# A two-block transformer kernel: the order of the four query blocks of each pair of heads, 128, 256, 384, 512 keys against 512, 128, 384, 256

## The reference, cut to what matters

```python
def fox_attention(q, k, v, log_f):
    ...
        s = jnp.einsum('bqhd,bkhd->bhqk', q_i, k).astype(jnp.float32) * scale
        s = s + c_i[..., :, None] - c_keys[:, :, None, :]
        s = jnp.where((k_pos[None, :] <= q_pos[:, None])[None, None], s, NEG_INF)
        p = jax.nn.softmax(s, axis=-1)
        return jnp.einsum('bhqk,bkhd->bqhd', p.astype(v.dtype), v)

def chunked_rel_attention(q, k, v, rel_bias):
    ...
    s = s + bias[None, :, None]
    s = jnp.where(valid[None, None, :, None, :], s, NEG_INF)
    p = jax.nn.softmax(s, axis=-1)
    o = jnp.einsum('bhnqk,bnkhd->bnqhd', p.astype(v.dtype), v_band)
```

## Time and profile before

| what | value |
|---|---|
| median of 3 runs | 1558.02 us (1558.0 to 1559.74) |
| profiled execution | 1563.09 us, span in the trace 1561.3 us |
| TensorE matmul busy | 1515.5 us, 97% of the span |
| VectorE, ScalarE, GpSimd busy | 54%, 39%, 15% of the span |
| stage of the 32 blocks on TensorE | from 157.2 us to 253.7 us of the span |

### The profile page before, as it was taken

The page is one execution under the profiler, slowest core; times in us unless marked ns, Lnnn a source line. Parts: engine busy times, 40 slices in busy tenths (PEclk is TensorE's granted clock), DMA queues, the critical chain, the costliest instruction groups (busy, mean ns, idle before and its releaser), DMA issues.

```text
span 1561.3 us, 21409 instructions
## 1 busy us (share of the span) xinstructions
PE 1515.5 (97%) x7988; PEld 1235.7 (79%) x7988; DVE 850.1 (54%) x1104; ACT 602.0 (39%) x923; POOL 240.3 (15%) x266
## 2 busy tenths in 40 slices
PE   9999988999998999999999899999999999999998
PEld 6787667887887888888888588888887788888887
DVE  6433564527545543433323786756876776767323
ACT  6222554643244322222323543335764433333222
POOL 0200000024014100000000554554542000000000
PEclk9999899999999999999999999999999999999999
DMA  5532002431112223333232123222002333232321
GB/s 166 190 97 92 1 2 64 153 108 54 55 55 81 81 81 107 93 96 108 81 107 90 50 77 108 81 98 91 2 1 82 96 91 107 81 107 82 109 105 54
DMA packets 152809, 132.22 MB, mean 85 GB/s; under 512 B 6300, under 2 KB 137628, under 8 KB 152740
## 3 DMA queue, kind: packets, MB, share of 16 engines
q1 hardware_dynamic: 150836, 128.11, 26.5%
q0 software_dynamic: 848, 3.17, 0.6%
q10 hardware_dynamic: 1056, 0.00, 0.0%
HBM read 129.15 MB, written 2.12 MB: 84 GB/s over the span
## 4 chain that ended last, share of the span: by engine, by line
PE 85%; DVE 5%; POOL 3%; ACT 3%; issue 3%; DMA 0%; ACTq 0%; SPq 0%; DVEq 0%; POOLq 0%
PE ps L1797 25%; PE ps L1798 25%; PE ps L1799 25%; PE ps L2048 2%; POOL other_stats L774 2%; PE ps L2161 1%; POOL x_t L722 1%; PE ps L2143 1%; PE ps L459 1%; PE ps L2058 1%; DVE a_lo L1281 1%; PE ps L1985 1%; ACT work L914 1%; PE ps L2014 0%; ACT w_hi L800 0%
## 5 line engine op out<-in xcount | busy, mean ns | idle before, releaser
L1797 PE MATMUL ps<-a_hi,w_hi 128*128 128x512 f32 (+2 forms) x1656 | 645.4, 390 | 14.8 <-DVE a_lo L1281 5.7
L1799 PE MATMUL ps<-a_hi,w_lo 128*128 128x512 f32 (+2 forms) x1656 | 639.9, 386 | 0.0
L1798 PE MATMUL ps<-a_lo,w_hi 128*128 128x512 f32 (+2 forms) x1656 | 639.8, 386 | 0.0
L1797 PEld LDWEIGHTS ps<-a_hi,w_hi 128*128 128x128 f32 (+1 forms) x1656 | 311.3, 188 | 87.9 <-issue 10.2
L1799 PEld LDWEIGHTS ps<-a_hi,w_lo 128*128 128x128 f32 (+1 forms) x1656 | 311.5, 188 | 64.0
L1798 PEld LDWEIGHTS ps<-a_lo,w_hi 128*128 128x128 f32 (+1 forms) x1656 | 311.6, 188 | 62.1 <-issue 0.7
L800 ACT ACTIVATE w_hi<-raw 128x2048 fp32r<-128x2048 f32 x118 | 225.8, 1913 | 348.5 <-PE ps L1799 346.4
L1233 DVE TENSOR_TENSOR w_lo<-raw,w_hi 128x2048 fp32r<-128x2048 f32 x94 | 215.3, 2290 | 245.0 <-ACT w_hi L800 244.7
L727 POOL TENSOR_TENSOR w_lo<-raw,w_hi 128x2048 fp32r<-128x2048 f32 x24 | 110.6, 4609 | 452.9 <-ACT w_hi L800 452.9
L1654 DVE TENSOR_TENSOR arena<-ps,rstd 128x512 f32<-128x512 f32 x88 | 60.2, 689 | 166.3 <-PE ps L1799 159.9
L1724 DVE RECIPROCAL rstd<-std 128x512 f32<-128x512 f32 x24 | 80.5, 3353 | 26.3 <-ACT std L1147 26.3
(11 more groups left out here) (242 smaller groups left out, 1459.3 us busy)
## 6 DMA issues: line engine op xcount, KB each, us to landing
raw<-in_w_gate_up SPq DMA_DIRECT2D x44, 512.0 KB, 4.6
raw<-in_ffn_w_up SPq DMA_DIRECT2D x44, 512.0 KB, 4.6
raw<-in_attn_w_in SPq DMA_DIRECT2D x36, 512.0 KB, 4.4
raw<-in_w_in SPq DMA_DIRECT2D x24, 512.0 KB, 4.7
raw<-in_w_down SPq DMA_DIRECT2D x22, 512.0 KB, 4.0
raw<-in_ffn_w_down SPq DMA_DIRECT2D x22, 512.0 KB, 4.0
raw<-in_w_mem_kv SPq DMA_DIRECT2D x16, 512.0 KB, 4.2
raw<-in_w_out SPq DMA_DIRECT2D x8, 512.0 KB, 3.9
```

What stands on the lines that cost most here:

```text
L1797: pe.matmul(dst, s_hi, m_hi, start=start, stop=False, skip_group_check=across)
L1798: pe.matmul(dst, s_hi, m_lo, start=False, stop=False, skip_group_check=across)
L1799: return pe.matmul(dst, s_lo, m_hi, start=False, stop=stop, skip_group_check=across)
```

## The change

One line decides which query block a number b stands for. Before, the four numbers of a pair of heads stand for i = 0, 1, 2, 3; now for i = 3, 0, 2, 1. Everything else of a block (keys, PSUM region, bias slice, place of the result) follows from i and moves with it; banks and slots still follow b.

```diff
             def __init__(self, b):
-                self.b, self.decays, self.p, self.i = b, b < 16, b % 16 // 4, b % 4
+                self.b, self.decays, self.p, self.i = b, b < 16, b % 16 // 4, (3, 0, 2, 1)[b % 4]
                 self.n, self.slot = (self.i + 1) * 128, 2 * (b % 2)
```

## The result

The changed kernel takes 1565.82 us (median of 5 runs, 1564.69 to 1566.54) against 1558.02 us of before (5 runs, 1557.78 to 1559.74): a ratio of 1.0045, 95% interval 1.003 to 1.006. It is slower by 7.8 us in this comparison; in a second one by 5.6 us (1565.82 against 1560.27, ratio 1.0038, 1.0025 to 1.0052, 23 runs of before from 1557.41 to 1564.23). I had forecast 1559.2, no measurable change, and a range up to 1562.3: wrong.

A forecast was written before the change was run, and what follows sets the result against it. TensorE, busy 97%, was taken to bound the kernel: bias pairs lose 1.5 us, decays pairs gain 0.2, head, middle and tail gain 0.1, so 1.2 us later, 1559.2 us from a median of 1558.02; range 1556.4 to 1562.3.

The forecast's parts named there:

- What bounds the stage, and the intervals: TensorE bounds; intervals from a block's scores (S) to the preceding block's values (V) each lose 0.11 us.
- the walk: TensorE's timeline reckoned piece by piece: decays pair 11.64 us (gain 0.09), bias pair 11.17 us (loss 0.49).
- V0's new wait: Bias pairs: values of the 128-key block wait some 0.8 us on ACT's copy, which they did not before.
- The mechanism: Two long intervals that ran side by side now stand in a row: 3.79 + 4.58 of a bias pair's 11.17 us.
- the head of the stage: Stage start: 512-key scores first, at low clock until 168.1 us; first transposes at 162.5, first pair takes 19.35 us.
- head, middle and tail together: Stage's first pair, pair between decays and bias, and last pair: together to gain 0.1 us.
- the rival of the early clock: Head of the stage: clock rises at about 161 us and stays, 1.2 us faster than before, 1556.8; chance 0.17.
- The rival of the low clock: Stage: clock stays low longer or falls again in longer waits, 4.6 us per low bias pair, 1563.8; chance 0.14.

The follow-up runs named there:

- Swap32: Kernel before with block order 128, 256, 512, 384 keys in both halves: 1560.19 us, ratio 0.9998.
- from128: Kernel before with block order 128, 384, 256, 512 keys, the changed kernel's cycle begun with its 128-key block: 1565.71 us, ratio 1.0027.
- before_2: The kernel before, unchanged, traced again: 1560.96 us.
- before_warm: Kernel before plus ten unread matmuls of 512 columns in TensorE's two gaps ahead of the stage: 1559.82 us, ratio 0.9992.
- rot: Kernel before with block order 256, 384, 512, 128 keys, the same cycle begun one block later: 1559.69 us, ratio 1.0002.
- again: The changed kernel, unaltered, run once more beside the kernel before: 1565.82 us, ratio 1.0038.
- filled pair: Kernel before and changed kernel, both with unread matmuls ahead of the stage and where V waits: 1557.72 and 1563.87 us.
- after_fed: Changed kernel plus unread matmuls: ten ahead of the stage, eight ahead of the first transposes, three to five where V waits: 1563.87 us, ratio 1.0021.
- after_3: The changed kernel, unaltered, traced again: 1564.76 us.
- before_fed: Kernel before plus unread matmuls: ten ahead of the stage, one ahead of the first transposes, three where V waits: 1557.72 us, ratio 0.9995.
- mix: Kernel before with order 128, 256, 512, 384 keys in the decays half and 256, 384, 512, 128 in the bias half: 1559.3 us, ratio 0.9991.

## Why the prediction was wrong

*What bounds the stage, and the intervals: right.* Each price of the walk came out. Predicted and measured: S2 to V0 with the bias 3.79 and 3.79, S3 to V1 4.58 and 4.58, with decays 3.99 and 4.00, 4.85 and 4.85; a decays pair 11.64 and 11.66, the pair between the halves 11.37 and 11.41, a bias pair 11.17 and 11.20, from the last T3 to `mem_k` 10.15 and 10.18. Only the first T3 came earlier than reckoned, 4.6 us behind the first scores and not 5.3. V0's new wait was to be 0.8 and is 0.79, V1's 1.6 and is 1.60.

*The mechanism: right, and tested.* Swap32, which keeps the two big scores in neighbouring steps, has bias pairs of 10.9 to 11.0 us; from128, another start of the changed cycle, has 11.20.

*The step that failed is the head of the stage,* and with it the sum. I took the low clock of the earlier trace rows, 158.0 to 168.1, as a property of the place and gave the changed kernel the same one; 253.69 us, with which I compared, held 10 us of it. The other traces show that it is one launch's: none, 3.4, 6.8 or 10.2 us in that place. Without it before needs about 92.6 us for the stage (before_2 has 94.0, less 0.64 in its pair of 11.32 us and 0.74 in its tail, both under low clock; before_warm, with none, has 92.7, rot 92.5) and the change 94.8 (again has 96.3, less 1.55 up to its second pair, which took 17.83 us where 4.62 to the first T3 and one pair of 11.66 make 16.28). So the order costs 2.2 us and not 1.2; in the filled pair 2.8 with the filling's 0.6. In the prediction's terms: the bias pairs lose 1.5 us and the decays pairs gain 0.2, as reckoned, but head, middle and tail together were to gain 0.1 and lose about 0.8 at the upper level. The low clock made the head of before, cheap at the upper level, look 3.8 us dearer in the one trace that I had. The same step turned the rival of the early clock round: its first pair is about right (16.9 us reckoned, 16.4 in after_fed), but it was set against a before at low clock, and so came out 1.2 us faster where the order is 2.2 us slower. That the head's 19.35 us met 19.27 in the first trace after is luck: the stretch of low clock was 6.8 us there and not 10, it lay at 164 to 171, and the first T3 came 0.7 us earlier.

*The rival of the low clock: right in kind.* The clock did fall inside the stage behind the longer waits, in stretches of 3.4 us that cost 1.1 to 1.6 us each (a bias pair of 12.26 in place of 11.20 in the first trace after, 12.79 in after_3), not for a whole pair of heads at 4.6 us. Seven traces with the new bias cycle and its waits unfilled hold 8 low stretches behind 210 us (one, in from128, of 10 us), eight with another bias order 3. That points to the waits as a cause, but swap32 waits 1.54 us in V1 and has none, so it isn't shown. The mean over the traces above, 3.3 us between L2022 and L1797, takes in 2.2 of order and 1.1 of clock.

*The range failed for a second reason.* The three runs of before that I had were 1.7 us apart; 23 were 6.8 us apart. My base of 1558.02 us was the median of three launches among the quickest; that of 23 is 1560.27. Of the 6.6 us between my 1559.2 and the measured 1565.82, then, 2.3 lie in the base, 1.0 in the stage (2.2 for 1.2), 2.0 go with the lower clock of the change's launches, which my sum had at nothing (the low clock was a rival, at 0.14), and 1.3 stay open.

*What stays open.* The medians stand 5.6 us apart. 2.2 us are the order's, at the upper level. Another 2.0 go with granted clock, 0.9916 against 0.9937 on average, and with it goes the spread, 6.8 us over the launches of before and 2 over ten of the change: nine of the 23 launches of before ran at 0.996, and none of the change's above 0.993. Why the change's launches never reached that is not shown; the fed pair has the same, six of eleven launches of before_fed at 0.997, none of after_fed above 0.996. That a shift of 2 to 3 us moves later gaps to where the clock falls more often would fit it, and wasn't tested. The last 1.3 us, the difference between 3.5 at equal clock and 2.2, aren't placed either: stretches that lie in the stage may cost more than those behind it, or the straight line is too coarse. Filling the gap ahead of 43.5 us was not tried.

## What to carry to other kernels

In a pipeline over engines read the interval from a producer to the consumer that waits behind it, not durations, and ask which long intervals run side by side: an order that sets two of them in a row lengthens the cycle though no instruction changed. A low-clock stretch in a trace belongs to that launch; work out both orders at the upper level first, and add the clock as a spread for both, not as a fixed cost in one place. And take more than one trace of each kernel before explaining a difference of a few tenths of a per cent, and compare the launches at equal granted clock.

## What the runs showed that I had not expected

The granted clock fell in places ahead of and behind the stage from launch to launch: at 44 to 48 us in four of the eighteen traces, the head of the stage for 0 to 10.2 us. The part from `mem_k` to the end, the same code in all, took 1304.8 us with 6.8 us at the lower level (before_fed, mix) and 1308.0 to 1308.5 with 20.4 (before_2, again, rot, after_fed). The list of launches with their mean granted clock says more about such a gap than a few traces: it parts what an order costs at equal clock from what the clock adds.
